# A MoE decoder layer on one core: VectorE's weight copy and row turn in swapped order

## The reference, cut to what matters

```python
# scores, grouping and top-8 routing give top_idx, top_w for each of the N = 1024 tokens
buf_tok, buf_w, block_e = ...          # tokens sorted by expert, in blocks
def expert_block(args):
    tok, e = args
    xb = x_pad[tok]
    return swiglu(xb, w_eg[e], w_eu[e], w_ed[e])   # silu(x @ gate) * (x @ up) @ down
y = lax.map(expert_block, (buf_tok.reshape(n_blocks, MOE_BLK), block_e)).reshape(P, D)
y = y * buf_w[:, None]
routed = jnp.zeros((N + 1, D)).at[buf_tok].add(y)[:N]
return routed + swiglu(xf, w_sg, w_su, w_sd)
```

## Time and profile before

| | us |
|---|---|
| median of 3 runs | 1437.5 |
| lowest, highest | 1436.06, 1438.08 |
| profiled execution: device time | 1437.38 |
| profiled execution: span of the core | 1435.5 |

### The profile page before, as it was taken

One profiled execution on the slowest core, in us unless ns is written; L12 is line 12 of the kernel. 1 busy time (PEld: TensorE's weight loads), 2 busy tenths in 40 slices (PEclk: granted clock), 3 DMA queues, 4 the chain that ended last, 5 costly groups with the idle time before them and its releaser, 6 DMA issues.

```text
span 1435.5 us, 23858 instructions
## 1 busy us (share of the span) xinstructions
PE 1403.0 (98%) x6055; PEld 585.2 (41%) x6056; DVE 1011.6 (70%) x1998; ACT 442.1 (31%) x648; POOL 621.7 (43%) x626
## 2 busy tenths in 40 slices
PE   7999999999999979999999999999999999999997
PEld 3456465565565433333333333333333333333333
DVE  2344454544444569899898899898899899899932
ACT  1223333233234212333333333333333333333330
POOL 3010312302212424556556656655656655655631
PEclk9999999999999989999999999999999999999999
DMA  9511102112019438989899989888999999998927
GB/s 345 188 65 56 54 28 81 45 38 81 30 68 364 162 103 317 310 287 362 286 366 344 314 286 341 249 266 268 316 338 380 327 322 299 314 330 271 348 38 208
DMA packets 74638, 330.07 MB, mean 230 GB/s; under 512 B 14647, under 2 KB 16184, under 8 KB 48932
## 3 DMA queue, kind: packets, MB, share of 16 engines
q1 hardware_dynamic: 45140, 249.62, 45.6%
q0 software_dynamic: 29456, 79.93, 22.7%
HBM read 282.74 MB, written 65.11 MB: 242 GB/s over the span
## 4 chain that ended last, share of the span: by engine, by line
PE 92%; DMA 4%; DVE 2%; issue 1%; SPq 0%; ACT 0%; DVEq 0%; POOLq 0%; POOL 0%; ACTq 0%
PE psP L733 57%; PE psW L733 31%; PE psW L946 2%; DMA area<-x_dram 2%; DMA wts<-in_w_in_dram 1%; PE psW L784 1%; DMA x_dram<-area,sidx 1%; PE psT L826 1%; PE psT L810 1%; DMA wts<-in_w_exp_up_dram 0%; DVE bias L1615 0%; PE psT L741 0%; PE psW L761 0%; DVE area L1422 0%; DVE st_s L1432 0%
## 5 line engine op out<-in xcount | busy, mean ns | idle before, releaser
L733 PE MATMUL psP<-wts,bias 128*64 (+1 forms) x1296 | 576.0, 597 | 11.7 <-DVE bias L1615 8.9
L733 PE MATMUL psP<-area,bias 128*64 128x512 f32 x1264 | 561.4, 597 | 0.0
L1615 DVE STREAM_TRANSPOSE bias<-area 32x256 f32<-32x256 f32 x1264 | 549.4, 435 | 16.3
L733 PE MATMUL psW<-wts,area 128*64 (+2 forms) x1592 | 426.3, 592 | 2.1 <-ACT wts L1246 1.6
L733 PEld LDWEIGHTS psP<-wts,bias 128*64 128x64 f32 (+1 forms) x1296 | 172.9, 138 | 348.1 <-issue 348.1
L733 PE MATMUL psP<-wts,area 128*128 128x512 f32 (+1 forms) x704 | 287.7, 560 | 5.9 <-DMA wts<-in_w_in_dram 4.4
L733 PEld LDWEIGHTS psW<-wts,area 128*64 128x64 f32 (+1 forms) x1592 | 150.7, 147 | 250.3 <-issue 248.5
L689 POOL DMA_INDIRECT out_dram<-area,sidx x79 | 115.7, 1464 | 259.3 <-ACT area L1238 207.2
L689 POOL DMA_INDIRECT x_dram<-area,sidx x79 | 197.3, 2498 | 28.2 <-issue 25.0
L1652 DVE COPY area<-wts 128x4096 f32 x79 | 182.3, 2308 | 16.3 <-issue 14.9
L733 PEld LDWEIGHTS psP<-wts,area 128*128 128x128 f32 x704 | 131.1, 191 | 135.9 <-issue 126.5
(11 more groups left out here) (223 smaller groups left out, 805.5 us busy)
## 6 DMA issues: line engine op xcount, KB each, us to landing
wts<-in_w_exp_gate_dram SPq DMA_DIRECT2D x64, 1024.0 KB
wts<-in_w_exp_up_dram SPq DMA_DIRECT2D x64, 1024.0 KB
wts<-in_w_exp_down_dram SPq DMA_DIRECT2D x64, 1024.0 KB
wts<-in_w_in_dram SPq DMA_DIRECT2D x4, 2048.0 KB, 17.5
area<-in_x_dram SPq DMA_DIRECT2D x8, 512.0 KB
wts<-in_w_out_dram SPq DMA_DIRECT2D x1, 4096.0 KB, 19.5
area<-u_dram SPq DMA_DIRECT2D x16, 256.0 KB, 2.8
xn_dram<-area POOLq DMA_DIRECT2D x8, 512.0 KB
```

The costliest lines, as they stand in the source:

```text
L733: return nc.tensor.matmul(out_, lhsT, rhs, start=start, stop=stop)
L1615: i = V.transpose(xT[par][q * QUAD:(q + 1) * QUAD, :, a * QUAD:(a + 1) * QUAD], rows[:, :, q * QUAD:(q + 1) * QUAD])
```

## The change

In each iteration of the routed loop VectorE copies the gate/up weights of job r+2 first and turns its rows second.

```diff
                 for k in ks:
                     r = i * 2 + (2 + k)
                     h_mul(r + NSH, k, tab_w[:, bass.ds(r, 1)])
+                    copy_gu(r + 2, k)
                     turn_x(r + (NSH + 2), k, i + 3)
-                    copy_gu(r + 2, k)
```

## The result

| | before | after |
|---|---|---|
| median, us | 1437.4 | 1472.24 |
| lowest, highest | 1436.06, 1438.08 | 1471.23, 1472.71 |
| profiled execution, device time | 1437.38 | 1472.42 |
| its span | 1435.5 | 1470.6 |

The ratio is 1.0243 with a 95% interval of 1.0229 to 1.0256: the changed kernel is 35 us slower. The forecast was 1439.4 in a range of 1436.5 to 1446, so it was wrong, and by far. The granted TensorE clock was 0.995 of full speed in both profiled executions. One execution of experiment 6 took 5234.54 us, for a reason that was not looked for; the ratio given there leaves it out.

What follows compares the result with a forecast made beforehand. The prediction took PE alone to bound the routed loop, with VectorE close behind. It summed 1437.38 + 0 (register work) + 0 (GpSimd) + 2.0 (late weights) = 1439.4 us, in a range of 1436.5 to 1446.

Steps and rivals of the forecast that it cites:

- What bounds the kernel: Routed loop: PE alone sets the 10.82 us per job, with 0.0 us idle before gate/up; VectorE is busy 10.15.
- Part 1: VectorE in the loop: the copy's 2.4 us register work loses cover, h_mul keeps 0.95 us before t_h; cost 0.
- the last paragraph: Signs expected in the next profile, among them about 0.7 us idle before VectorE's copy and h_mul without idle time.
- S: The end of silu in a job of the routed loop, from which the prediction counts its times in us.
- part 3: Near the loop's end: copies wait for weights 5.4 us earlier; PE waits 1.95 us once, within 0 to 4.5.
- Part 2: GpSimd in the loop: the gather's issue ends about 3.8 us behind the turn's end, before 4.6; cost nothing.
- Rival B: Routed loop: VectorE becomes the bound through h_mul behind the transposes, over two jobs; 22 us, 1459 us; chance 0.14.
- Rival C: Routed loop: the copy waits 1.06 us for the gather's issue in every job; 4 us, 1441 alone; chance 0.06.
- Rival A: Near the loop's end: nothing is late, job 74's weights had landed by 1324.5; 1437.4 us; chance 0.20.
- D: Faster: scatter issues no longer meet the copy, GpSimd comes free earlier, start-up or tail gains; 1434 us; chance 0.05.

Runs made afterwards that it cites:

- experiment 6: Kernel before, with PE's two register loads for the weight slots moved ahead of t_h: 1434.9 us, ratio 0.9981.
- experiment 4: Kernel before, with a second multiplication into a scratch buffer between silu and h_mul in the routed loop: 1493.05 us, ratio 1.0391.
- experiment 1: Kernel after, with PE's two register loads for the weight slots moved ahead of t_h: 1441.98 us, 1.0038 of the kernel before.
- experiment 3: Kernel after, with the copy placed between two halves of eight transposes each: 1437.83 us, 1.0006 of the kernel before.

## Why the prediction was wrong, point by point

**What bounds the kernel: right, and read too far.** PE had 0.0 us of idle time before gate/up. I took the nearest event ahead of it, t_h, for the point that h_mul must meet. An idle time of 0.0 says that PE was not late; it doesn't say by how much.

**Part 1, the register work's size: right.** The copy was expected 2.4 us behind h_mul's start and came 2.49 behind (814.56 - 812.07). The idle time before it was 1.82 us, not the "about 0.7" of the last paragraph; the 1.7 of Part 1 was the right number. "h_mul starts about 1.0 us later", at S + 1.25, held for every second job, where it is mostly 1.33 us or a little more behind silu; in the others VectorE has caught up, and it is 0.24 to 0.50.

**Part 1, the slack: this is the step that failed.** "h_mul ends at S + 1.9 and t_h needs it at S + 2.85 ... 0.95 us are left". The point to meet was not t_h but gate/up at S + 14.04 - 10.82 = S + 3.22, with the time in front of it that PE's sequencer needs. From S + 1.9 there are 1.32 us; a job with k = 0 needs 1.94, or 2.34 with the branch (experiment 4). So 0.6 or 1.0 us were missing. The prediction's own steps with this one number put right: transposes end at S + 12.1, h_mul at S + 12.75, gate/up at S + 14.69 or S + 15.09 instead of S + 14.04. That is 0.65 or 1.05 us late per two jobs, 0.85 in the mean, 29 us over the 34 pairs; the chain's rows gave 30.2. With the 2.0 us of part 3 the sum would have been some 1468 us.

The number could be had. In the start-up of the kernel before, the chain has h_mul's end at 554.00 and gate/up at 556.06, 2.06 us behind, with 1.58 us of "issue" between t_h and gate/up (the rows under experiment 6). Nothing covers PE's sequencer there, so that row is its price. (The branch's 0.4 us more could not be read there.)

**Part 2, GpSimd: right but for a size.** The gather's index copy was expected at 0.2 us and its issue 1.2 us behind the turn's end, stretched to the end of the weight copy that it meets. GpSimd of the kernel after:

```profile
824.12 0.18 POOL L663 COPY gidx<-area 128x1 int32 x1 [4.04 <-DVE bias L1615]
825.20 3.12 POOL L666 DMA_INDIRECT area<-xn_dram,gidx  x1 [0.90 <-POOL gidx L663]
```

The index copy took 0.18 us and the issue came 1.26 us behind the turn's end (825.20 - 823.94). It lasted 3.12 us, where 1.05 had been usual, and ended 0.9 us behind the copy's end (825.11 + 2.29 = 827.40), 4.4 us behind the turn's end and not 3.8. As forecast it cost nothing.

**Part 3, late weights: right in kind.** It forecast one wait near the end, 1.95 us within 0 to 4.5. With the loop at its old pace (experiment 1) the copy of that job came at 1325.57, where 1326.7 was forecast, and the next was held as well; the two made gate/up 0.61 and 1.82 us late, where 1.95 and 0 were forecast. In the kernel after, the last jobs cost 4.2 us in all.

**Rival B: the right mechanism with the wrong threshold.** It named the loop over two jobs, and what closed it. Its point of decision, 0.95 us, was taken over from Part 1, so it got a chance of 0.14 and the worst single values as its only way in. Its price of 22 us was worked out from 0.6 us over per pair; 0.89 was measured (22.53 less 21.64, twice 11.264 in the mean).

**Rival C falls as a cause, but its mechanism is there.** After the change many copies start inside a gather's issue, 19 of them; in experiment 1 it is 45. This is one of GpSimd in experiment 1, whose copy at 825.93 stands in the rows above:

```profile
825.51 2.84 POOL L666 DMA_INDIRECT area<-xn_dram,gidx  x1 [0.89 <-POOL gidx L663]
```

GpSimd issued first, at 825.51. The copy still started at 825.93, took its usual 2.30 us, and it was the issue that became longer. Another pair of the same run went the other way:

```profile
976.92 1.05 POOL L666 DMA_INDIRECT area<-xn_dram,gidx  x1 [0.89 <-POOL gidx L663]
```

```profile
977.49 2.57 DVE L1658 COPY area<-wts 128x4096 f32 x1 [1.11 <-DMA wts<-in_w_exp_up_dram]
```

Here the issue kept its 1.05 us and the copy took 0.28 us more. What differs is the copy's start within the issue. In 38 of the 45 it is 0.00 to 0.50 us behind the issue's start: the copy takes 2.29 to 2.32 us, and the issue ends 0.12 us behind it. In the other 7 it is 0.57 to 0.79 us: the issue takes 1.05, and the copy takes 2.35 to 2.57 and ends 3.14 us behind the issue's start in each. By the rule of the Trainium skill ("SBUF — State Buffer", section "Who interferes with whom") whichever issues first keeps the shared ports for its whole length and the other blocks. The trace agrees with the exclusion but not with the whole length: the copy is held by 0.28 us at most, where rival C took 1.06, and only from the middle of the issue on. The prediction's row could not show this: the issue at 819.38 is a scatter's (L689), and it is a gather's (L666) that the copy meets after the change. None of the 35 us is in it: copies take 2307 ns in the mean after and 2309 before.

**Rival A** (nothing late) and **D** (faster) fall with the result.

## What to carry to other kernels

Slack is measured up to the instruction that must not be late, and through all that its sequencer does between the wait and that instruction: register loads, address arithmetic, assertions and branches have no row as work of the engine. Where an engine shows no idle time, look for the place in the same trace where the same code runs without cover (start-up or tail): the "issue" piece of the chain there is the price. And loads of registers that don't depend on the awaited data belong ahead of the wait; here that alone made the kernel before 0.2% faster and cut what VectorE's changed order costs from 35 to some 8 us (experiment 1 is 5.2 us above the kernel before beside it, experiment 6 2.5 below).

## What the runs showed of the hardware that was not expected

- From h_mul's end to the next gate/up matmul PE takes 1.70 to 1.97 us with two register loads of 0.30 us behind the wait, and 2.30 to 2.36 us with a loop branch among them (experiment 4 and the kernel after). For a t_h of two short matmuls (0.44 us) that is mostly sequencer.
- A multiplication of 128 x 256 took 1353 ns with a bf16 output and 672 ns with an f32 output, both written in strided order from the same inputs. In a pair of them the second started about 1.0 us after the first, not 1.35, and was recorded with some 0.84 us, where 0.67 is usual.
- VectorE's register work of the next copy began while some five of the 16 transposes were still to end, and eight transposes (3.55 us) are enough to hide it (experiment 3); one multiplication of 0.67 us is not.
- A gather's issue on GpSimd and a weight copy on VectorE exclude each other for part of the issue only. A copy that starts up to 0.50 us behind the issue's start takes its usual 2.3 us, and the issue is stretched from 1.05 to as much as 2.92; one that starts 0.57 to 0.79 us behind it leaves the issue as it is and itself takes up to 2.57 us (45 pairs in experiment 1).
